# Quadrant matmuls in a block inverse, and attention values in column tiles, in a two-block float32 transformer kernel

## What is computed

```python
a_mat = jnp.where(strict, jnp.einsum('bnhid,bnhjd->bnhij', kbeta, kc) * decay, 0.0) \
    + jnp.eye(C, dtype=q.dtype)
rhs = jnp.concatenate([vc * bc, kbeta * jnp.exp(gc)[..., None]], axis=-1)
sol = lax.linalg.triangular_solve(a_mat, rhs, left_side=True, lower=True, unit_diagonal=True)
```

## Time and profile before

| | us |
|---|---|
| median of 3 runs | 1675.0 (1673.0 to 1675.16) |
| profiled execution | 1673.16 |
| its span, first to last instruction | 1671.4 |
| PE busy | 1610.6 (96%) |
| DVE busy | 1028.8 (62%) |
| ACT busy | 888.7 (53%) |
| POOL busy | 65.8 (4%) |

### The profile page before, as it was taken

The page is one execution under the profiler, slowest core; times in us unless marked ns, Lnnn a source line. Parts: engine busy times, 40 slices in busy tenths (PEclk is TensorE's granted clock), DMA queues, the critical chain, the costliest instruction groups (busy, mean ns, idle before and its releaser), DMA issues.

```text
span 1671.4 us, 23416 instructions
## 1 busy us (share of the span) xinstructions
PE 1610.6 (96%) x9618; PEld 1408.8 (84%) x9618; DVE 1028.8 (62%) x1555; ACT 888.7 (53%) x1400; POOL 65.8 (4%) x58
## 2 busy tenths in 40 slices
PE   7999989999998999999999999989999999999999
PEld 7989977998987778889988888879888888778887
DVE  6876674897566665555685655555555555764544
ACT  4984473596446455445535544444554446754442
POOL 0013000011200000000000000000000001000000
PEclk9999999999999999999999999999999999999999
DMA  6624214552412565555422656534565553245652
GB/s 222 203 79 141 76 68 155 145 178 65 144 52 101 189 217 186 181 192 159 153 99 76 201 179 198 178 126 151 177 220 183 178 175 127 76 152 178 200 177 101
DMA packets 205690, 252.99 MB, mean 151 GB/s; under 512 B 19216, under 2 KB 185360, under 8 KB 205456
## 3 DMA queue, kind: packets, MB, share of 16 engines
q1 hardware_dynamic: 205584, 251.50, 46.9%
HBM read 250.43 MB, written 1.05 MB: 150 GB/s over the span
## 4 chain that ended last, share of the span: by engine, by line
PE 82%; DVE 9%; ACT 7%; issue 1%; DMA 1%; SPq 0%; POOL 0%; DVEq 0%; ACTq 0%; POOLq 0%
PE bank L795 79%; ACT arena L1471 4%; DVE weights_rest L2017 3%; DVE arena L2165 2%; ACT weights_high L1471 1%; PE bank L1246 1%; DMA ring<-in_w_in 1%; PE bank L852 1%; ACT L1466 1%; ACT L1471 1%; DVE xT_rest L2412 1%; PE bank L1183 0%; DVE x L2381 0%; DMA vec<-in_vec 0%; DVE small L2336 0%
## 5 line engine op out<-in xcount | busy, mean ns | idle before, releaser
L2017 DVE TENSOR_TENSOR weights_rest<-ring,weights_high 128x1024 fp32r<-128x1024 f32 (+3 forms) x414 | 477.2, 1197 | 180.1 <-ACT weights_high L1471 178.5
L1471 ACT ACTIVATE weights_high<-ring 128x1024 fp32r<-128x1024 f32 (+3 forms) x414 | 400.1, 1020 | 131.1 <-PE bank L795 115.3
L795 PE MATMUL bank<-weights_high,xT_high 128*128 128x512 f32 (+2 forms) x880 | 334.9, 385 | 8.6 <-DVE xT_rest L2412 3.5
L795 PE MATMUL bank<-weights_high,xT_rest 128*128 128x512 f32 (+2 forms) x816 | 306.1, 375 | 0.0
L1471 ACT ACTIVATE arena<-bank 128x512 f32<-128x512 f32 (+4 forms) x293 | 139.7, 497 | 301.0 <-PE bank L795 292.3
L795 PE MATMUL bank<-xT_high,weights_high 128*128 128x256 f32 (+1 forms) x944 | 277.7, 294 | 3.9 <-DVE xT_rest L2111 2.4
L795 PE MATMUL bank<-xT_rest,weights_high 128*128 128x256 f32 (+1 forms) x944 | 271.1, 287 | 0.0
L795 PE MATMUL bank<-xT_high,weights_rest 128*128 128x256 f32 (+1 forms) x912 | 261.7, 287 | 0.0
L795 PE MATMUL bank<-weights_rest,xT_high 128*128 128x512 f32 (+2 forms) x696 | 261.0, 379 | 0.0
L795 PEld LDWEIGHTS bank<-weights_high,xT_high 128*128 128x128 f32 x880 | 166.1, 189 | 40.8 <-issue 4.8
L795 PE MATMUL bank<-arena 128*128 128x128 f32 (+3 forms) x1416 | 180.8, 292 | 16.7 <-ACT arena L1471 11.4
(11 more groups left out here) (186 smaller groups left out, 1954.1 us busy)
## 6 DMA issues: line engine op xcount, KB each, us to landing
ring<-in_w_in SPq DMA_DIRECT2D x36, 1024.0 KB, 5.2
ring<-in_ffn_w_gate SPq DMA_DIRECT2D x71, 512.0 KB, 4.0
ring<-in_ffn_w_up SPq DMA_DIRECT2D x71, 512.0 KB, 4.9
ring<-in_ffn_w_down SPq DMA_DIRECT2D x34, 1024.0 KB, 4.9
ring<-in_w_out SPq DMA_DIRECT2D x22, 1024.0 KB, 4.9
ring<-in_w_in_a SPq DMA_DIRECT2D x11, 1024.0 KB, 5.3
ring_more<-in_ffn_w_down SPq DMA_DIRECT2D x10, 1024.0 KB, 4.9
ring_more<-in_ffn_w_gate SPq DMA_DIRECT2D x17, 512.0 KB, 4.0
```

The source lines that it names most:

```text
L795: return eng.matmul(o, a, b, start=first, stop=last)
L1471: return eng.activation(dst, src, func, **kw_)
L2017: TTs(rest_slot(b)[:, part], raw_slot(b)[:, part], high_slot(key)[:, part].bitcast(F32), ALU.subtract).then_inc(*dv.mark(("rest", key, z)))
```

## The change

Three edits. In the list, gz's first projection is put ahead of vT. In the delta rule, tri and trid up to level 32 are done in the two diagonal blocks of 64 alone: each 128x128x128 product becomes two of 64x64x64, one in rows and columns 0 to 63 and one in 64 to 127, and ACT's copy and DVE's subtractions are likewise two instructions on 64 partitions, each of 4x64 elements. In the attentions that are not wide, each head multiplies its own 64 value columns into its own 64 partitions of the same bank columns; the two heads take turns, and DVE reads the result with one instruction.

```diff
--- before.py
+++ after.py
@@ -163,7 +163,7 @@
         out += [proj("lx", 0), ("abt", l), proj("lx", 1), proj("mq", 0), proj("gq", 0), ("lru", l), proj("mq", 1)]
         out += [proj("gq", 1), ("lru_b", l), proj("mkv"), ("silu", l, 0), proj("gk", 0), ("lru_c", l), proj("mkr")]
         out += [proj("gk", 1), ("l2", l, 0), proj("gv", 0), ("silu", l, 1), ("decay", l), proj("lz", 0), proj("gv", 1)]
-        out += [("decay_b", l), ("l2", l, 1), proj("lz", 1), ("silu", l, 2), ("mla_norm", l), ("vT", l), proj("gz", 0)]
+        out += [("decay_b", l), ("l2", l, 1), proj("lz", 1), ("silu", l, 2), ("mla_norm", l), proj("gz", 0), ("vT", l)]
         out += [("gdn_a", l, n) for n in range(2)]
         rots = [("rot", l, i) for i in (4, 0, 1, 2, 3)]
         beside = {2: ([("uq", l, 0)], [("uq", l, 1)]), 4: ([("uq", l, 2)], [("uq", l, 3)]),
@@ -615,6 +615,10 @@
                 v = v.rearrange(f"p ({' '.join(names)}) -> p {' '.join(names)}", **dict(zip(names[1:], dims[1:])))
             return v
 
+        def quarters(s):
+
+            return [(slice(0, P), slice(0, P))] if s == LEVELS[-1] else [(slice(d, d + 64), slice(d, d + 64)) for d in (0, 64)]
+
         def bcast(ap, n):
             return ap.unsqueeze(2).to_broadcast([ap.shape[0], ap.shape[1], n])
 
@@ -981,7 +985,9 @@
                 pe.wait_ge(*at(("T", l, n, s // 2)))
                 b = group(("U", l, n, s))
                 for h in range(4):
-                    ins = mm(b[:, h * P:h * P + P], AM[:, n, h, :], TT[:, n, 0, h, :])
+                    for at_rows, at_cols in quarters(s):
+                        o = b[at_rows, h * P:h * P + P][:, at_cols]
+                        ins = mm(o, AM[:, n, h, at_rows], TT[:, n, 0, h, at_cols])
                 ins.then_inc(*pe.mark(("U", l, n, s)))
 
             def st_trid(st):
@@ -997,10 +1003,12 @@
                 for z in range(2) if s < LEVELS[-1] else (1,):
                     b = group(("D", l, n, s, z))
                     for h in range(4):
-                        if z == 0:
-                            ins = mm(b[:, h * P:h * P + P], TT[:, n, 1, h, :], U[:, n, h, :])
-                        else:
-                            ins = mm(b[:, h * P:h * P + P], U[:, n, h, :], TT[:, n, 1, h, :])
+                        for at_rows, at_cols in quarters(s):
+                            o = b[at_rows, h * P:h * P + P][:, at_cols]
+                            if z == 0:
+                                ins = mm(o, TT[:, n, 1, h, at_rows], U[:, n, h, at_cols])
+                            else:
+                                ins = mm(o, U[:, n, h, at_rows], TT[:, n, 1, h, at_cols])
                     ins.then_inc(*pe.mark(("D", l, n, s, z)))
 
             def st_gdn_u(st):
@@ -1190,11 +1198,14 @@
                 for t in range(NT):
                     nk = kw(name, t) // P
                     pe.wait_ge(*at(("pts", name, hp, t)))
-                    for f in range(2):
-                        h = 2 * hp + f if a["wide"] else hp
-                        for kt in range(nk):
-                            ins = mm(b[:, f * S + t * P:f * S + t * P + P], a["v"][:, kt, h * P:h * P + P],
-                                     a["pt"][:, t, kt, f, :], kt == 0, kt == nk - 1)
+                    for f, kt in ([(f, kt) for f in range(2) for kt in range(nk)] if a["wide"] else [(f, kt) for kt in range(nk) for f in range(2)]):
+                        if a["wide"]:
+                            h = 2 * hp + f
+                            o, values = b[:, f * S + t * P:f * S + t * P + P], a["v"][:, kt, h * P:h * P + P]
+                        else:
+                            d = 64 * f
+                            o, values = b[d:d + 64, t * P:t * P + P], a["v"][:, kt, hp * P + d:hp * P + d + 64]
+                        ins = mm(o, values, a["pt"][:, t, kt, f, :], kt == 0, kt == nk - 1)
                 ins.then_inc(*pe.mark(("pv", name, hp)))
                 if (name[0], hp) == ("m", 0):
                     kept.clear()
@@ -1763,7 +1774,8 @@
                     return
                 if s > 2:
                     ac.wait_ge(*at(("D", l, n, s // 2, 1)))
-                copy(U[:, n], g, ps(g, 4, P), ("Us", l, n, s))
+                for at_rows, at_cols in quarters(s):
+                    copy(U[at_rows, n, :, at_cols], g, ps(g, 4, P)[at_rows, :, at_cols], ("Us", l, n, s))
 
             def st_gdn_o(st):
                 _, l, n = st
@@ -2265,7 +2277,9 @@
                 for z in range(2) if s < LEVELS[-1] else (1,):
                     g = ("D", l, n, s, z)
                     dv.wait_ge(*at(g))
-                    TTs(TT[:, n, z], TT[:, n, z], ps(g, 4, P), ALU.subtract).then_inc(*dv.mark(("T", l, n, s), frees=g))
+                    for at_rows, at_cols in quarters(s):
+                        T = TT[at_rows, n, z, :, at_cols]
+                        TTs(T, T, ps(g, 4, P)[at_rows, :, at_cols], ALU.subtract).then_inc(*dv.mark(("T", l, n, s), frees=g))
                 if s == LEVELS[-1]:
                     dv.wait_ge(*at(("T", l, n, s)))
                     dv.wait_ge(*at(("AM", l, n, s)))
@@ -2357,21 +2371,17 @@
                 _, name, hp = st
                 g = ("pv", name, hp)
                 dv.wait_ge(*at(g))
-                v = ps(g, 2, S)
                 if name[0] == "m":
                     l = int(name[1])
                     dv.wait_ge(*at(("gate", l, "mz", hp)))
                     m = mixed[:, 4 + 2 * hp:6 + 2 * hp, :]
-                    TTs(m, v, m, ALU.mult).then_inc(*dv.mark(("mb", name, hp), frees=g))
+                    TTs(m, ps(g, 2, S), m, ALU.mult).then_inc(*dv.mark(("mb", name, hp), frees=g))
+                elif name[0] == "e":
+                    eng.tensor_copy(mix2[:, 6 + hp, :], ps(g, S)).then_inc(*dv.mark(("mb", name, hp), frees=g))
                 else:
-                    for f in range(2):
-                        half = slice(64 * f, 64 * f + 64)
-                        if name[0] == "e":
-                            eng.tensor_copy(mix2[half, 6 + hp, :], v[half, f, :]).then_inc(*dv.mark(("mb", name, hp), frees=g))
-                        else:
-                            dv.wait_ge(*at(("gate", "pb", hp // 2)))
-                            m = mix2[half, hp, :]
-                            TTs(m, v[half, f, :], m, ALU.mult).then_inc(*dv.mark(("mb", name, hp), frees=g))
+                    dv.wait_ge(*at(("gate", "pb", hp // 2)))
+                    m = mix2[:, hp, :]
+                    TTs(m, ps(g, S), m, ALU.mult).then_inc(*dv.mark(("mb", name, hp), frees=g))
 
             def add_half(st, t, scale):
```

## The result

The changed kernel takes **1658.87 us** (median of 4 runs, 1657.45 to 1661.63) against 1674.59 for the kernel before in the same comparison: ratio 0.9912, 95% interval 0.9897 to 0.9926. That is 15.7 us less, where 16.0 were forecast. The profiled execution is the slowest of the four (1661.63, span 1659.9), 11.5 us under the one of before.

A forecast was written before the change was run, and what follows sets the result against it. PE was taken to bound the kernel, busy 96% of the span. Block inverse 12.8, values 2.8 and swap 0.4 sum to 16.0 us off 1675.0, giving 1659.0 us, range 1652 to 1668.

The forecast's parts named there:

- The slot of a pair: Block inverse, levels 2 to 32: 240 pairs at 0.058 us instead of 0.108 per instruction, gaining 12.1 us per layer.
- rival (a): Block inverse: slots do not shrink, pairs keep 0.108 us, and the kernel gets slower, 1679.6 us; chance 0.10.
- Changing the tile shape: Block inverse on PE: 11 tiled runs per layer lose 0.35 us each on entering and leaving, 3.9 us per layer.
- The wait at tri(0,64): Level 32: PE waits 1.8 us per layer for DVE, whose halved reads stand behind rope steps.
- rival (b): The granted clock falls after PE's wait at level 32 or the swap's idle time: 1662 or 1666 us; chance 0.20.
- The forecast's 12.8 for this part: Block inverse, two layers: 12.1 - 3.9 - 1.8 = 6.4 us gained per layer, 12.8 us in all.
- Values: Products with values in the memory attention and last attention: pairs halve their time, 2.8 us gained in sum.
- The swap: gz ahead of vT: the chain behind is DVE's, so 0.1 us gained, 0.3 in the second layer, 0.4 in sum.
- apart in both: Block inverse: the two products were taken as diagonal quadrants, apart in rows and in columns, and assumed to pair.

The follow-up runs named there:

- e11_fill: The changed kernel with 22 throwaway 128x128 matmul instructions put into PE's wait ahead of tri(0,64): 1654.46 us.
- e3_inverse: The changed kernel with swap and values taken back, so the kernel before with only the block inverse edited: 1664.31 us.
- e1_swap: The kernel before with one edit, gz's first projection ahead of vT: 1674.92 us, ratio 1.0003.
- e8_compact: The changed kernel with both 64-blocks held in the same columns, a smaller level 64, gz behind vT, rope steps two and three at level 32: 1647.68 us.
- e4_rots23: The changed kernel with two rope steps beside chunk 0 at level 32 and three beside chunk 1, instead of three and two: 1654.36 us.
- e10_compact32: e8_compact with three rope steps beside chunk 0 and two beside chunk 1, as before: 1653.24 us.
- e6_unpaired: e3_inverse with the loops over heads and blocks exchanged, so that eight instructions in a row go to the same columns: 1668.08 us.

## Why the prediction was right

The total was right to 0.1 us, and the experiments show that this is partly luck: terms of both signs were off.

- **The slot of a pair** (0.058): right. In the blocks, 24 pairs and one change of tile shape take 1.55 us; 24 x 0.058 = 1.39. The main gain was where the forecast put it, and rival (a), slots of 0.108, is out.
- **Changing the tile shape** (0.35 for a run): too high. The distance from block to block fell by 1.03 us, the slots give 24 x 0.050 = 1.20, so a run costs 0.17 to 0.18, half. I had added the losses read at the scores and at the decay, 0.15 on entering and 0.20 on leaving. The starts in the block at 133.90 us show 0.05 and 0.10: the second pair begins 0.106 us after the first instead of 0.058, and the projection 0.16 after the last pair. Eleven runs: 2.0 us per layer instead of 3.9. The Trainium skill (TensorEngine Tiling (Array Packing), Key Properties) says that a change of the tiling mode drains the array; the trace agrees that it costs, with 0.17 us.
- **The wait at tri(0,64)** (1.8): the mechanism was right, its size 1 us short. Halves at 0.44 each and ropes in the way were foreseen; that POOL's masks hold the rope's instructions was not, although the row of before at 176.08 us, 0.64 instead of 0.42, showed it.
- **The low clock**, rival (b), given 0.20: it happened, at level 32 as described, in both layers. e11_fill prices it at 4.4 us in the changed kernel, with its three low stretches; e3_inverse has one in each layer, 1.6 us each by its trace beside that of before, 3.2 in all. The forecast had kept it out of its sum. Slots 12.1, less 2.0, less 2.8 is 7.3 per layer; 14.6 less 3.2 to 4.4 is 10.2 to 11.4 us, and e3_inverse measured 10.0 (8.0 to 12.2). The forecast's 12.8 for this part was too much.
- **Values** (2.8): 3.7 by the traces, 6.0 by the median. A memory product gained 0.57 to 0.91 where 0.52 stood, again because the change of shape was priced at 0.35. The rule of the Trainium skill (TensorE: Matmul & The Clock Gate, What overlaps and what doesn't) that loads run beside a matmul only where the row groups differ, which by the forecast would leave 1 us, does not hold here: the two heads share all rows, and so do the two blocks of the inverse, which I had not seen; both keep full pace.
- **The swap** (0.4): 0.6 the other way, which is nothing that can be told (e1_swap). As argued, the chain behind it is DVE's; the low clock moves with the idle time, so that the 0.3 us for the second layer is not there.
- **What was misread**, in the text ahead of the prediction and in it: the blocks' products as quadrants, "apart in both". Columns alone part them. That they pair rested on the rows of column tiles, which cover this, so the number stood on the right row for the wrong reason; e8_compact shows that quadrants run at the same pace.

So two steps failed that met in the total: the term of 3.9 us per layer for tile changes, where 2.0 was lost, and the low clock, which the sum kept at nothing. 2 x 1.9 us too much in the one nearly equals the 3.2 to 4.4 us left out in the other. The waits, 2 us too short, and the swap were made up by the values, by their 6.0 us in the median; the traces show 3.7 of these, and where the other 2 us come from stays open. That the total fits to 0.1 us is luck for a second reason: the four runs behind the median lie between 1657.45 and 1661.63.

## What to carry to other kernels

Where a block matrix leaves half of the columns of a product empty, two of the halves run side by side and a float32 instruction of 64 columns costs 0.029 us in a pair; but look at what the new shape does to the readers. Here e8_compact gave another 11 us: 4.5 came with one rope step fewer ahead of DVE's reads (e4_rots23), the other 6.7 with both halves in the same columns, a smaller last level and gz put back together. A wait in a stretch of short matmuls costs its length and can bring low clock behind it: ahead of tri(0,64) the waits of 2.8 us (changed kernel, e3_inverse) and 1.70 us (e10_compact32) did in both layers, those of 2.08 us (e6_unpaired) in one, that of 1.20 us (e4_rots23) in none. So price both.

## What the runs showed that I had not expected

- Tiles that share all rows still pair (24 pairs, 0.058 us apart), and a run of four instructions for one tile, then four for the other, overlaps as well as turns (1.11 against 1.09 us for 16). With runs of eight 48 took 2.12 us instead of 1.62.
- 22 throwaway matmuls in a wait made the kernel 4 us faster (1654.46 against 1658.87), with the granted clock at 1.00 instead of 0.50 behind it.
- A DVE instruction on two SBUF operands that starts while POOL's mask runs ends 0.27 to 0.29 us after it: 0.72, 1.17, 1.17 and 1.46 us instead of 0.42 in four cases.
